# Latent attention in a two-block network: one weight split a turn between rope and outputs, outputs cast from the product bank, softplus moved into the first feed-forward

## The reference

```python
q = (cq @ w_uq).reshape(bsz, seq, MLA_HEADS, QK_NOPE + QK_ROPE)
q_nope, q_pe = q[..., :QK_NOPE], _rope(q[..., QK_NOPE:], cos, sin)
...
s = (jnp.einsum("bqhd,bkhd->bhqk", qn, k_nope)
     + jnp.einsum("bqhd,bkd->bhqk", qp, k_pe)).astype(jnp.float32) * scale
p = jax.nn.softmax(jnp.where(allowed[None, None], s, -jnp.inf), axis=-1).astype(v.dtype)
o = jnp.einsum("bhqk,bkhd->bqhd", p, v)
y = o.reshape(bsz, seq, MLA_HEADS * V_HEAD) @ w_o          # then layer norm "ln2" and ff1
...
log_a = -RG_C * r * jax.nn.softplus(-lam)                  # second block: one value per channel
```

## Time and profile before

| | us |
|---|---|
| median of 3 runs | 825.92 |
| the profiled execution | 827.24 |
| its span in the trace | 825.0 |
| PE busy | 781.7 (95%) |
| DVE busy | 601.1 (73%) |
| ACT busy | 402.8 (49%) |
| mean granted clock of PE | 0.977 |

### The profile page before, as it was taken

The page is one execution under the profiler, slowest core; times in us unless marked ns, Lnnn a source line. Parts: engine busy times, 40 slices in busy tenths (PEclk is TensorE's granted clock), DMA queues, the critical chain, the costliest instruction groups (busy, mean ns, idle before and its releaser), DMA issues.

```text
span 825.0 us, 12430 instructions
## 1 busy us (share of the span) xinstructions
PE 781.7 (95%) x5172; PEld 713.5 (86%) x5172; DVE 601.1 (73%) x798; ACT 402.8 (49%) x485; POOL 32.0 (4%) x58
## 2 busy tenths in 40 slices
PE   6999999999999999969999999999599978999996
PEld 5999898899988898848988999988499958999985
DVE  5785888877776885777988767766879865656643
ACT  5454235453444324554354434442768966554631
POOL 0000000000000010000000000001400004000000
PEclk9999999999999999989999999999699999999999
DMA  8976448897776624163588987763344642754101
GB/s 315 361 275 221 153 164 321 333 349 280 274 266 258 236 77 141 53 250 131 184 319 325 344 296 274 268 244 121 101 155 135 234 168 104 255 203 155 52 26 51
DMA packets 26263, 174.72 MB, mean 212 GB/s; under 512 B 2912, under 2 KB 3296, under 8 KB 6880
## 3 DMA queue, kind: packets, MB, share of 16 engines
q1 hardware_dynamic: 26208, 173.93, 57.9%
HBM read 172.87 MB, written 1.05 MB: 211 GB/s over the span
## 4 chain that ended last, share of the span: by engine, by line
PE 82%; DVE 10%; ACT 6%; issue 2%; DMA 0%; POOL 0%; DVEq 0%; POOLq 0%; SPq 0%; ACTq 0%
PE bank L492 11%; PE bank L494 11%; PE bank L493 11%; PE Y L574 9%; PE Y L576 9%; PE Y L573 9%; DVE w_low L1278 4%; ACT w_high L936 2%; PE bank L831 2%; PE bank L833 2%; PE bank L832 2%; PE Y L597 2%; PE bank L520 1%; PE bank L518 1%; PE bank L519 1%
## 5 line engine op out<-in xcount | busy, mean ns | idle before, releaser
L1278 DVE TENSOR_TENSOR w_low<-raw,w_high 128x2048 fp32r<-128x2048 f32 (+2 forms) x129 | 285.5, 2228 | 66.4 <-ACT w_high L936 65.8
L936 ACT CAST w_high<-raw 128x2048 fp32r<-128x2048 f32 (+2 forms) x129 | 237.9, 1859 | 72.5 <-DMA raw<-weights 66.2
L492 PE MATMUL bank<-xT_h,w_high 128*128 128x256 f32 x736 | 209.0, 284 | 2.9 <-DVE w_low L1276 2.9
L493 PE MATMUL bank<-xT_l,w_high 128*128 128x256 f32 x736 | 208.8, 284 | 0.0
L494 PE MATMUL bank<-xT_h,w_low 128*128 128x256 f32 x736 | 208.8, 284 | 0.0
L492 PEld LDWEIGHTS bank<-xT_h,w_high 128*128 128x128 f32 x736 | 141.6, 192 | 4.5 <-DVE w_low L1276 3.2
L493 PEld LDWEIGHTS bank<-xT_l,w_high 128*128 128x128 f32 x736 | 141.5, 192 | 1.0
L494 PEld LDWEIGHTS bank<-xT_h,w_low 128*128 128x128 f32 x736 | 141.6, 192 | 0.0
L573 PE MATMUL Y<-w_high,hT_h 128*128 128x512 f32 x324 | 128.6, 397 | 2.5 <-DVE hT_l L1294 2.5
L574 PE MATMUL Y<-w_low,hT_h 128*128 128x512 f32 x324 | 129.2, 399 | 0.0
L576 PE MATMUL Y<-w_high,hT_l 128*128 128x512 f32 x324 | 102.3, 397 | 0.0
(11 more groups left out here) (227 smaller groups left out, 1258.5 us busy)
## 6 DMA issues: line engine op xcount, KB each, us to landing
raw<-weights SPq DMA_DIRECT2D x151, 1024.0 KB, 5.2
rows<-rows_in SPq DMA_DIRECT2D x9, 512.0 KB, 7.2
raw<-weights SPq DMA_DIRECT2D x4, 768.0 KB, 4.3
raw<-weights SPq DMA_DIRECT2D x4, 512.0 KB, 3.9
raw<-weights SPq DMA_DIRECT2D x2, 896.0 KB, 4.8
x<-x_in SPq DMA_DIRECT2D x2, 512.0 KB, 4.2
kT<-rows_in SPq DMA_DIRECT2D x2, 512.0 KB, 6.7
out<-x SPq DMA_DIRECT2D x4, 256.0 KB, 2.0
```

The costliest lines, as they stand in the source:

```text
L492: mm(dst, high, xh[:, kt, :], start=kt == 0, stop=False)
L493: mm(dst, high, xl[:, kt, :], start=False, stop=False)
L936: nc.scalar.copy(w_high[:, n % RING, start:COLS[n]], raw[:, s % RAW, start:COLS[n]]).then_inc(w_high_ready, 1)
L1278: tt(w_low[:, n % RING, start:COLS[n]], slot[:, start:COLS[n]], f32(w_high[:, n % RING, start:COLS[n]]), ALU.subtract).then_inc(raw_done, 1)
```

## The change

It does four things in the latent attention:

1. The weight splits. Before, DVE and ACT split in turns 0 to 3, behind the outputs, q2, q3, d0 with d1, d2 with d3 (ACT without q2, which it casts ahead of the turns). Now DVE splits one piece a turn in turns 0 to 4 (q2, q3, d0, d1, d2), between rope and outputs; ACT is one piece ahead (q3, d0, d1, d2, d3), between the PT copies and the outputs' high part. d3's low part goes in front of the layer norm.
2. The outputs. ACT casts the high part straight from the bank, DVE subtracts from the same bank, and this second step evacuates it. The copy to `stage` and the signal `o_low` are gone; `down` waits for the two banks instead.
3. Softplus goes to group 10 of the 16 of ff0, and the exponential that it needs goes on ACT ahead of "ln0".
4. `silu_of_c(2)` goes behind the layer norm "ln2".

The block attention "mo" keeps its outputs by way of `stage`.

```diff
--- before.py
+++ after.py
@@ -225,7 +225,7 @@
     "row_max": {"mla": TB * HEADS, "mo": TB * HEADS},
     "probs": {"mla": TB * HEADS, "mo": TB * HEADS},
     "o_high": {"mla": HEADS, "mo": HEADS},
-    "o_low": {"mla": HEADS, "mo": HEADS},
+    "o_low": {"mo": HEADS},
 }
 
 
@@ -562,7 +562,10 @@
                     else:
                         pe.wait_ge(hidden_low, nth("hidden_low", phase, g - FILL * (phase in ("ff0", "ff1"))))
                 else:
-                    pe.wait_ge(S["o_low"], nth("o_low", phase, GT * g + GT - 1))
+                    for h in (GT * g, GT * g + 1) if phase == "mla" else ():
+                        await_evacuated(pe, phase, "O", h)
+                    if phase == "mo":
+                        pe.wait_ge(S["o_low"], nth("o_low", phase, GT * g + GT - 1))
                     th, tl, t0 = head_tiles(phase, GT * g)
                 await_piece(n)
                 for t in range(GT):
@@ -1036,17 +1039,23 @@
                                                 ACT.Exp, bias=nmx[:, c:c + 1], accum_out=rsum[:, c:c + 1])
                 last.then_inc(evacuates(phase, "S", h), 1)
 
-            def outputs_high(phase, heads):
+            def transposed_high(phase, heads):
                 for h in heads:
                     await_product(act, phase, "PT", h)
                     if h >= 2:
                         await_product(act, phase, "O", h - 2)
                     nc.scalar.copy(buf_b[:, h % 2, 0:3 * P], bank_of(phase, "PT", h)[:, 0:3 * P])\
                         .then_inc(evacuates(phase, "PT", h), 1)
+
+            def outputs_high(phase, heads):
                 for h in heads:
-                    await_evacuated(act, phase, "O", h)
+                    if phase == "mla":
+                        await_product(act, phase, "O", h)
+                    else:
+                        await_evacuated(act, phase, "O", h)
                     th, _, t = head_tiles(phase, h)
-                    nc.scalar.copy(th[:, t, :], stage[:, h % 2, 0:SEQ]).then_inc(S["o_high"], 1)
+                    src = bank_of(phase, "O", h)[:, 0:SEQ] if phase == "mla" else stage[:, h % 2, 0:SEQ]
+                    nc.scalar.copy(th[:, t, :], src).then_inc(S["o_high"], 1)
 
             norm_transposed("init")
             split_ahead(("sc", "C", 0), 0)
@@ -1067,6 +1076,8 @@
                 await_evacuated(act, "sc", "B", g)
                 hidden_high_of("sc", g)
             split_ahead(("sc", "down", MXG - 1), FILL)
+            act.wait_ge(lam_exp_in, 1)
+            nc.scalar.activation(prm[:, 7, :], prm[:, 6, :], ACT.Exp, scale=-1.0).then_inc(lam_exp, 1)
             norm_transposed("ln0")
             feed_forward("ff0")
             split_ahead(("ff0", "down", FFG - 1), 3)
@@ -1105,8 +1116,6 @@
             keys(2)
             keys(3)
             split_ahead(("mla", "q", 2), 0)
-            act.wait_ge(lam_exp_in, 1)
-            nc.scalar.activation(prm[:, 7, :], prm[:, 6, :], ACT.Exp, scale=-1.0).then_inc(lam_exp, 1)
             for g in range(MXG + 1):
                 heads = (GT * g - 2, GT * g - 1)
                 if g:
@@ -1119,9 +1128,10 @@
                     if g == 0:
                         latent_values(1)
                 if g:
+                    transposed_high("mla", heads)
+                split_ahead(("mla", "q", 3), g)
+                if g:
                     outputs_high("mla", heads)
-                if g < MXG:
-                    split_ahead(("mla", "q", g), max(2, g + 1))
             tanh_of_c(2)
             split_ahead(("mla", "down", MXG - 1), FILL)
             norm_transposed("ln2")
@@ -1236,6 +1246,7 @@
                         await_product(act, "gate", 1, n)
                         nc.scalar.copy(z[:, 1, n * 512:(n + 1) * 512], bank_of("gate", 1, n)[:, :]).then_inc(evacuates("gate", 1, n), 1)
                 if g:
+                    transposed_high("mo", heads)
                     outputs_high("mo", heads)
             split_ahead(("mo", "down", 0))
             act.wait_ge(shift_in, 16 * 5)
@@ -1419,6 +1430,8 @@
                         split_ahead((phase, "up", 0 if g < FILL - 1 else g), AHEAD, min(g, 1) if g < FILL - 1 else 0)
                     if g >= FILL:
                         hidden_low_of(phase, g)
+                    if (phase, g) == ("ff0", FFG - 6):
+                        softplus_of_lambda()
 
             def softmax(phase, heads):
                 for h in heads:
@@ -1441,19 +1454,18 @@
                         ts(p, p, rinv[:, c + b:c + b + 1], None, ALU.mult).then_inc(S["probs"], 1)
 
             def outputs_low(phase, heads):
-                for h in heads:
+                for h in heads if phase == "mo" else ():
                     await_product(dve, phase, "O", h)
-                    o, st = bank_of(phase, "O", h)[:, 0:SEQ], stage[:, h % 2, 0:SEQ]
-                    if phase == "mla":
-                        nc.vector.tensor_copy(st, o).then_inc(evacuates(phase, "O", h), 1)
-                    else:
-
-                        stt(out=st, in0=o, scalar=0.5, in1=o_gate(h), op0=ALU.mult, op1=ALU.mult)\
-                            .then_inc(evacuates(phase, "O", h), 1)
+                    stt(out=stage[:, h % 2, 0:SEQ], in0=bank_of(phase, "O", h)[:, 0:SEQ], scalar=0.5, in1=o_gate(h),
+                        op0=ALU.mult, op1=ALU.mult).then_inc(evacuates(phase, "O", h), 1)
                 for h in heads:
                     th, tl, t = head_tiles(phase, h)
                     dve.wait_ge(S["o_high"], nth("o_high", phase, h))
-                    tt(tl[:, t, :], stage[:, h % 2, 0:SEQ], f32(th[:, t, :]), ALU.subtract).then_inc(S["o_low"], 1)
+                    if phase == "mla":
+                        tt(tl[:, t, :], bank_of(phase, "O", h)[:, 0:SEQ], f32(th[:, t, :]), ALU.subtract)\
+                            .then_inc(evacuates(phase, "O", h), 1)
+                    else:
+                        tt(tl[:, t, :], stage[:, h % 2, 0:SEQ], f32(th[:, t, :]), ALU.subtract).then_inc(S["o_low"], 1)
 
             for b in range(TB):
                 low_transposed("init", b)
@@ -1607,14 +1619,11 @@
                     if g:
                         dve.wait_ge(rope_ready, g)
                     rope(g)
-                else:
-                    softplus_of_lambda()
+                split_ahead(("mla", "q", 2), g)
                 if g:
                     outputs_low("mla", heads)
-                if g < MXG:
-                    split_ahead(("mla", "q", g), max(2, g + 1))
+            layer_norms("ln2", "mla", 2, FILL, FILL)
             silu_of_c(2)
-            layer_norms("ln2", "mla", 2, FILL, FILL)
             feed_forward("ff1")
 
             layer_norms("ln3", "ff1", 0, 2, 2, lows=False)
```

## The result

| | before | after |
|---|---|---|
| median of 4 runs each | 826.07 (824.08 to 829.58) | 815.28 (814.22 to 815.88) |
| ratio, 95% interval | | 0.9866 (0.9844 to 0.9889) |
| the profiled execution | 827.24 | 815.88 |
| its span | 825.0 | 813.6 |
| mean granted clock of PE | 0.977 | 0.985 |

The forecast was 814.8 us in a range of 812.8 to 818.2; the time is 0.5 above it. I call this stretch A, and use it wherever a few tenths matter: the 1.3 us by which the changed kernel reaches the turns later were lost in the first 100 us, where both do the same work, and 1.5 us of difference between the two executions lies in the second block.

What follows compares the result with a forecast made beforehand. DVE's queue was taken to bound attention turns 3 and 4, making PE wait for probabilities. The turns give 11.1 us, other terms 0: 827.24 becomes 816.1, and 814.8 us against the median, 1.3 lower; range 812.8 to 818.2.

Steps and rivals of the forecast that it cites:

- The cause: Attention turns 3 and 4: DVE's weight splits delay the mask, so PE waits 3.14 and 3.84 us for probabilities.
- doesn't do what it says: Rival in the attention turns: probabilities are late for another reason than the split, gaps stay, 825.9 us; chance 0.03.
- The turn: Attention turns 2 and 3: without the extra split no wait for DVE, a turn bound by PE takes 9.65 us.
- Turn 4: Last attention turn: PE waits 0.3 and 0.6 us; the rest of the output projection starts at 364.8, 11.1 us less.
- The banks: Attention turns: O banks held until DVE's low part, T+4.2 and T+4.7, leaving 0.9 us before the next projection.
- Behind the turns: From turn 4 to layer norm ln2: DVE's outputs and three splits done by 372.7, PE 373.1; cost 0 to 2.3, taken 0.
- the last raw tile: Freed by d2's split in turn 4, 5.0 us to land, there at 367.8, 0.6 before ACT wants it.
- Softplus and silu: Softplus in ff0 (bounds 0 and 3.1 us) and silu behind ln2 (0 and 1.3): both taken as 0.
- The low clock in turn 4: Rival: the low clock stays in turn 4, costing 2.5 us more, 817.3 us; chance 0.10.
- The small new wait: Rival: O banks held too long, the ln2 chain or silu costs 1 to 2.3 us, about 816.8; chance 0.12.
- Late transfers: Rival on ACT in the turns: weights landing late hold its casts, 14.4 us in all, 829.2 us; chance 0.03.
- The median: Whole kernel: profiled execution 827.24 less 11.1 is 816.1; it lies 1.3 above the median, so 814.8 us forecast.

Runs made afterwards that it cites:

- e1: The kernel before with only the weight splits moved, on DVE and ACT; 816.48 us, ratio 0.9872 to before.
- e2: The changed kernel with the weight splits back in their old places and numbers, all else new; 823.68 us, ratio 0.9970 to before.
- e6: The changed kernel with four additional DVE operations as a delay ahead of the first mask of turn 3; 818.12 us, ratio 0.9868 to before.
- e7: The changed kernel with six additional DVE operations as a delay ahead of the first mask of turn 3; 821.27 us, ratio 0.9914 to before.
- e12: The changed kernel with DVE's split behind the outputs in turns 0 to 3, turn 4's left ahead; 815.38 us, ratio 0.9864 to before.
- e5: The changed kernel with only the direct outputs undone, going by way of stage again; 815.50 us, ratio 0.9875 to before.
- e8: The changed kernel with three row loads issued behind ff1's second weight and ACT's tanh behind its weight casts; 814.69 us, ratio 0.9870 to before.
- e3: The changed kernel with softplus back in turn 4, ahead of the split of d2; 815.60 us, ratio 0.9870 to before.
- e4: The changed kernel with silu of c back ahead of the layer norm; 817.20 us, ratio 0.9887 to before.
- e11: The changed kernel with each of DVE's splits behind the outputs, still one a turn; 821.62 us, ratio 0.9913 to before.

## Why the prediction was right, point by point

**The cause.** It named DVE's queue: the second split in front of the mask. That is shown from both sides. Moving the splits alone gives 9.14 of 11.16 (e1); with all else changed and the splits in the old place the gaps return (e2); a delay of known length put there brings back gap and low clock (e6, e7). That it is the second split is shown by e12: with one split a turn in the old place behind the outputs (but for the last), the gaps are 0.30 and 1.40, where e2, with the old places and numbers on DVE and ACT, has 2.60 and 4.13. The prediction calls the two long splits those of turn 3; they are d0 and d1, at the end of turn 2 ahead of the mask of turn 3, and no number hangs on the name. The rival "doesn't do what it says" falls with e1 and e2.

**The turn.** Predicted 9.65, measured 9.52 and 9.57. The model put DVE's low parts at T+4.72; they end at T+4.26 (336.59 + 0.76 - 333.09). The mask starts 0.14 to 0.15 behind the start of what follows the scores on PE (0.15 taken). The 9.65 was not bound by PE alone, as the prediction had it: from the start of the projection to PT of turn 2 it took 4.47 before (336.96 to 341.43) and takes 4.33 now (338.28 to 342.61), so 0.1 of it was a wait for DVE that the row doesn't show.

**Turn 4.** Predicted waits 0.3 and 0.6; the rows show none and 0.50. The first is there all the same, at about 0.2: PT starts at T+8.22, 0.14 behind DVE's first probabilities (359.71 + 0.55 = 360.26), and from the start of the output block to it PE takes 3.03 (357.37 to 360.40), where the next block, which nothing holds up, takes 2.84 (361.70 to 364.54). The ends of products are modelled, and the last one covers the wait in the view. The two PTs came at T+8.22 and T+9.25, predicted 8.2 and 9.2. From there to the rest of the output projection it took 4.33, against 0.4 + 2.8 + 1.3 = 4.5. The 0.2 in two turns and these 0.2, less 0.05 by which the second PT was later, make it 11.43 where 11.1 was predicted.

**The banks.** Held until T+4.26 in turn 1 and T+4.36 in turn 3 (355.79 + 0.75 less 352.18), wanted from T+5.19 (338.28 less 333.09): 0.8 to 0.9 to spare, predicted 0.9, and no wait. A cast out of a bank takes 0.39 (0.3 to 0.43 predicted). DVE's subtraction takes 0.42 out of a bank, in the bounds of 0.4 to 0.8 but below the 0.49 taken, which was half of a row of two with the pause between them. The Trainium skill ("VectorE: DVE Perf Modes", in the section on the TRN2 errata) gives a PSUM source 62 cycles more than an SBUF source; the trace doesn't agree for this operation, which reads one operand from the bank and one from SBUF and takes 420 ns by either way. e5 shows that the direct outputs are worth nothing in time, as the sum had it.

**Behind the turns.** This is the term that was mis-sized. I took 0 in bounds of 0 to 2.3 and called the last raw tile the tightest link, with 0.6 to spare. The tile was issued at 363.5, and ACT waited for it 1.28, to 370.46: 6.9 us and not 5.0, since three row loads of 512 KB issued in the 6 us before were still landing. In e8, with these loads issued later, it is 5.0. DVE waited 0.90 for the third split, and its sum came 8.85 behind the start of the rest of the output projection, where it was 8.49 before (384.37, less 375.88) and is 8.49 in e8. The cost is 0.27 to 0.36: by e8, and by that difference. So the right link was named; of the 1.3 on ACT 0.9 reached DVE and 0.3 PE. The prediction also misread: DVE's wait of 0.2 for PE stands before the second half of the layer norm (393.46). Before the first (384.37) DVE waited for nothing, since it came there straight from its last split. A draw it was, as 8.49 is also what PE needs in e8, where DVE does wait for it (0.77); the prediction took 8.3. The median of a transfer was the wrong number: what lands beside it at that moment has to be looked up.

**Softplus and silu.** Both hidden at their new places, as predicted. At the old place softplus costs 1.1 (e3). "Removing it there gives PE nothing by itself" was said of the kernel before, where DVE idled 3.09 behind softplus for PE's product; no run takes softplus alone out of it. In the new order d2's split stands behind softplus and frees the raw tile: in e3 ACT waits 2.37 for the next weight (1.28 after), DVE 1.82 for ACT (0.90 after), and PE 0.94 for `x`. Silu's 1.22 at its old place costs 0.7 (e4), which leaves 0.5 for the slack that was put at 0.4. These two, 1.8 together, are most of the 2.0 by which e1 falls short of the change.

**The rivals.** The low clock in turn 4 didn't come: 1.00 in all rows, with a wait of 0.50 as in turn 2 before. The small new wait came, at 0.3 instead of 1 to 2.3. Late transfers didn't hold ACT in the turns.

**The median.** The profiled execution gave 815.88 where 816.1 was worked out, and 815.28 is the median where 814.8 was; both agree to 0.5. That it is so close is in part luck. In A the turns gave 0.3 more than predicted and the layer norm took 0.3 of it back; outside A the changed kernel's execution lost 1.3 us ahead of T1 and won 1.5 in the second block, and neither was forecast.

## What to carry to other kernels

Where an engine's queue mixes work that another engine waits for with work that fills, give each turn one piece of the latter, and put it where the engine would otherwise wait for a third (here: for ACT's output cast) and not in front of the step that PE waits for; of two legal places in a turn one cost 2.0 us more in the turns, and 4.8 more through the ring of tiles. Follow a buffer that comes free all the way round (free, issue, landing, cast, split: about 9 us here) before moving what frees it, with the transfers that land beside it. Price an idle gap of PE at its length and, where the clock falls behind it, 1.6 to 2.4 us more (e6, e7, e11).
